# Gate and up products in two passes over a chunk, and new byte offsets for the low halves and the activations

## The reference, cut to what matters

```
def swiglu(x, w_gu, w_down):
    g, u = jnp.split(x @ w_gu, 2, axis=-1)
    return (jax.nn.silu(g) * u) @ w_down

for l in range(DEPTH):                       # DEPTH = 2
    f = swiglu(rms_norm(x, ffn1_pre_g[l]), ffn1_w_gu[l], ffn1_w_down[l])
    x = x + 0.5 * rms_norm(f, ffn1_post_g[l])
    ...                                      # hybrid mixer, then the second feed-forward
```

## Time and profile before

| | |
|---|---|
| median of 3 runs | 1475.48 us (1472.1 to 1476.35) |
| the profiled execution | 1471.1 us |
| its span, first to last instruction | 1469.0 us |
| TensorE busy | 1453.0 us, 99% of the span |
| VectorE busy | 1148.5 us, 78% |
| ScalarE busy | 767.2 us, 52% |
| DMA of the weight stream | 53.8% of 16 engines' span |
| mean granted TensorE clock | 0.994 |

### The profile page before, as it was taken

The page is one execution under the profiler, slowest core; times in us unless marked ns, Lnnn a source line. Parts: engine busy times, 40 slices in busy tenths (PEclk is TensorE's granted clock), DMA queues, the critical chain, the costliest instruction groups (busy, mean ns, idle before and its releaser), DMA issues.

```text
span 1469.0 us, 24487 instructions
## 1 busy us (share of the span) xinstructions
PE 1453.0 (99%) x8583; PEld 1266.1 (86%) x8583; DVE 1148.5 (78%) x1831; ACT 767.2 (52%) x1252; POOL 143.8 (10%) x140
## 2 busy tenths in 40 slices
PE   8999999999999999999999999999999999999999
PEld 7888889888888888889988888889988899888887
DVE  5777777878777777777787777878899987577876
ACT  6343476663434544337655434468498665453432
POOL 0000015200000000002420000020433310000000
PEclk9999999999999999999999999999899999999999
DMA  8665555546656666555555665656422356556652
GB/s 320 198 198 193 188 167 180 164 145 197 196 188 192 213 202 199 188 189 167 166 160 180 200 199 184 197 175 192 158 82 87 87 174 197 176 164 198 197 191 81
DMA packets 71361, 261.75 MB, mean 178 GB/s; under 512 B 8048, under 2 KB 8048, under 8 KB 71024
## 3 DMA queue, kind: packets, MB, share of 16 engines
q1 hardware_dynamic: 69984, 253.79, 53.8%
q10 hardware_dynamic: 1296, 6.85, 1.3%
HBM read 259.56 MB, written 1.05 MB: 177 GB/s over the span
## 4 chain that ended last, share of the span: by engine, by line
PE 92%; DVE 4%; ACT 2%; issue 1%; POOL 0%; DMA 0%; ACTq 0%; DVEq 0%
PE work L768 25%; PE work L769 13%; PE acc L481 9%; PE acc L483 9%; PE acc L482 9%; PE work L481 8%; PE work L483 7%; PE work L482 7%; DVE wlo L467 2%; PE work L1500 1%; PE acc L1529 1%; ACT whi L460 1%; PE acc L1565 1%; PE work L1501 0%; PE work L1488 0%
## 5 line engine op out<-in xcount | busy, mean ns | idle before, releaser
L467 DVE TENSOR_TENSOR wlo<-raw,whi 128x1024 fp32r<-128x1024 f32 x460 | 550.8, 1224 | 179.6 <-ACT whi L460 178.3
L768 PE MATMUL work<-xboth,whi 128*128 128x512 f32 x1600 | 564.2, 394 | 0.0
L460 ACT ACTIVATE whi<-raw 128x1024 fp32r<-128x1024 f32 x480 | 475.9, 1040 | 59.4 <-PE work L483 28.1
L769 PE MATMUL work<-xboth,wlo 128*128 128x256 f32 x1600 | 448.4, 280 | 0.0
L768 PEld LDWEIGHTS work<-xboth,whi 128*128 128x128 f32 x1600 | 300.8, 188 | 68.7
L769 PEld LDWEIGHTS work<-xboth,wlo 128*128 128x128 f32 x1600 | 299.8, 187 | 3.5
L846 ACT ACTIVATE sg<-sg 128x256 f32<-128x256 f32 x100 | 41.9, 419 | 474.6 <-DVE sg L887 474.6
L481 PE MATMUL acc<-whi,hhi 128*128 128x512 f32 x440 | 172.5, 392 | 0.0
L483 PE MATMUL acc<-whi,hlo 128*128 128x512 f32 x440 | 172.1, 391 | 0.0
L482 PE MATMUL acc<-wlo,hhi 128*128 128x512 f32 x440 | 171.1, 389 | 0.0
L481 PE MATMUL work<-xboth,whi 128*128 128x256 f32 x416 | 118.3, 284 | 0.0
(11 more groups left out here) (438 smaller groups left out, 2193.9 us busy)
## 6 DMA issues: line engine op xcount, KB each, us to landing
raw<-stream SPq DMA_DIRECT2D x480, 512.0 KB, 3.7
par<-pm ACTq DMA_DIRECT2D x2, 1644.5 KB, 7.4
pfa<-pf_a ACTq DMA_DIRECT2D x3, 516.0 KB, 3.7
pfb<-pf_b ACTq DMA_DIRECT2D x2, 516.0 KB, 8.4
x<-x_in SPq DMA_DIRECT2D x2, 512.0 KB, 5.9
out<-x SPq DMA_DIRECT2D x4, 256.0 KB, 2.0
par<-pm ACTq DMA_DIRECT2D x1, 820.0 KB, 4.3
pre<-pf_a ACTq DMA_DIRECT2D x1, 4.0 KB, 4.1
```

The lines of the kernel that those rows point to most:

```text
L460: nc.scalar.activation(chunk(whi, place, c)[:, cols], chunk(raw, place, c)[:, cols], ACT.Copy).then_inc(hi_ready, 1)
L467: nc.vector.tensor_tensor(chunk(wlo, place, c)[:, cols], chunk(raw, place, c)[:, cols], chunk(whi, place, c)[:, cols].bitcast(F32), ALU.su ...
L768: nc.tensor.matmul(o[:, :], hi[:, k * P:(k + 1) * P], xboth[:, k, :], start=k == 0, stop=False)
L769: m = nc.tensor.matmul(o[:, 0:S], lo[:, k * P:(k + 1) * P], xhi[:, k, :], start=False, stop=k == KD - 1)
```

## The change

Two edits. The loop of columns_of is cut in two: first the eight 512-column products of a chunk with the high weights, then the eight 256-column ones with the low weights. And unused 64-byte tensors are added or resized, so that each low part starts at another offset than its high part. From the sizes, the offsets modulo 128 after it are: whi 0, wlo 64, xboth (xhi and xlo) 0, hhi 0, hlo 64, yahi 0, yalo 64, mxhi 0, mxlo 64, and y5, cv and o at 64 as before. The number of instructions, the waits and the semaphore counts are the same.

```
@@ block_program, allocations @@
         whi = sb("whi", [P, RING * CH], F32R)
+        sb("low_line", [P, 16])
         wlo = sb("wlo", [P, RING * CH], F32R)
...
-        m1("hidden_line", [P, LINE])
+        m1("hidden_line", [P, 16])
         hhi = m1("hhi", [P, HELD, S], F32R)
+        m1("hidden_low_line", [P, 16])
         hlo = m1("hlo", [P, HELD, S], F32R)
...
-        m1("lru_line", [P, LINE])
-        yahi, yalo = m1("yahi", [P, AB, S], F32R), m1("yalo", [P, AB, S], F32R)
+        m1("lru_line", [P, 16])
+        yahi = m1("yahi", [P, AB, S], F32R)
+        m1("lru_low_line", [P, 16])
+        yalo = m1("yalo", [P, AB, S], F32R)
...
-        sb("state_line", [P, 16])
         y5hi, y5lo = sb("y5hi", [P, 4, S], F32R), sb("y5lo", [P, 4, S], F32R)
...
-        sb("mixed_line", [P, LINE // 2])
-        mxhi, mxlo = sb("mxhi", [P, KD, S], F32R), sb("mxlo", [P, KD, S], F32R)
+        sb("mixed_line", [P, 16])
+        mxhi = sb("mxhi", [P, KD, S], F32R)
+        sb("mixed_low_line", [P, 16])
+        mxlo = sb("mxlo", [P, KD, S], F32R)
@@ columns_of @@
                 for k in range(KD):
                     nc.tensor.matmul(o[:, :], hi[:, k * P:(k + 1) * P], xboth[:, k, :], start=k == 0, stop=False)
+                for k in range(KD):
                     m = nc.tensor.matmul(o[:, 0:S], lo[:, k * P:(k + 1) * P], xhi[:, k, :], start=False, stop=k == KD - 1)
                 m.then_inc(consumed, 1)
```

More of the change, by code:

```diff
@@ L38 @@
 VSTEPS = 49
-LINE = 32
 FFN_CHUNKS = 3 * FT
```

## The result

The changed kernel takes 1480.54 us, median of 8 runs, against 1473.0 us before, median of 8: a ratio of 1.0048, 95% interval 1.0037 to 1.0059. By the ratio it is 7.1 us slower; the prediction, 11.7 us faster and at most 1478, was wrong. (The 1464 us stood on a median before of 1475.48 us, of three runs; eight gave 1473.0.)

What follows compares the result with a forecast made beforehand. The prediction took TensorE's pace of starting products alone to bound the kernel. Its terms, -8.8 - 0.8 - 2.1 = -11.7 us, gave 1459.4 us in a profiled execution and 1464 us as a median, range 1452 to 1478.

Steps and rivals of the forecast that it cites:

- What bounds the kernel: Whole kernel: time comes only from TensorE's pace of starting products; other engines can follow a pace 3% higher.
- The offsets: All products: 512-column runs with moved and loaded operand both at 0 modulo 128 settle at 226.7 ns; unlike offsets may not.
- new first pass: Gate and up loop, eight 512-column products: 229.1 ns each, bounds 226.7 and 233.
- The second pass: Gate and up loop, 256-column products with low weights: 115.4 ns each, bounds 113.1 and 120.
- The pair: Gate and up, one 512- and one 256-column product: 344.5 ns against 350, -8.8 us; bounds -16.3 and +4.8.
- Down: Down and held products: like offsets stay like, so less is lost to settling, -0.8 us; bounds -1.7 and +6.2.
- tokens: 512-column products of tokens: two of three come from 233 to 226.7 ns, -2.1 us; bounds -3.2 and 0.
- channels: 256-column products of channels: possible gain of 5.0 us or loss of 2.7 us, taken as 0.
- y5, cv and o: These operands stay where they are; no time change was entered for their products.
- Products reach the best pace when the same kind follows itself: All products: best pace comes after three to seven of one kind; alternating 512 and 256 columns in gate and up prevents it.
- the slower one: Rival: low halves at 64 keep gate, up and down runs from settling, +7.9 us, 1483 us; chance 0.14.

Runs made afterwards that it cites:

- The series: Kernels with the whole computation left out: runs of products at chosen byte offsets, nothing on other engines; 512 columns took 226.7 to 233.3 ns a product.
- order, x -64: Kernel before with the two-pass loop, low halves at their high halves' offsets, xboth 64 bytes before the weights modulo 256: 1467.08 us, ratio 0.995.
- the locked kernel: Kernel before, one pass, low weights and activations 64 past the high weights, hidden high half 192 past, hidden low half at 0: 1465.6 us, ratio 0.9948.
- order, x +64: Kernel before with the two-pass loop, xboth moved by 64 bytes, each low half at its high half's offset: 1477.42 us, ratio 1.0022.
- order alone: Kernel before with the loop in two passes and all offsets as before: 1472.82 us, ratio 0.9991.

## Why the prediction was wrong, point by point

**What bounds the kernel** was right: TensorE's pace alone; no wait appeared, and the other engines followed a kernel 7.7 us faster without one.

**The offsets (the step that failed).** The prediction put down, output projections and the new first pass into one class: "moved and loaded operand both start at 0 modulo 128". The series know such a class modulo 256 only. From the sizes modulo 256, with whi put at 128 (the differences are what matters), hhi, hlo and mx lie at 128 too in the kernel before, xboth at 192 and y5, cv and o at 64; the change put xboth at 0 and the low halves at 192. So the first pass moves 0 and loads 128, half a period apart, and the series alone with these two offsets runs at 233.3 ns: the kernel has 233.4 where 229.1 was predicted (bounds 226.7 and 233). The second pass moves 0 and loads 192; its series runs at 117.8, the kernel at 117.6, predicted 115.4. The pair came to 351.0 where 344.5 was predicted and 349.8 measured before: +2.0 us for -8.8, inside the bounds of the term.

**Down.** "Like offsets stay like offsets" pairs a moved operand with the weights loaded for the next product. Of the operands that a product itself multiplies, two of three pairs come 64 apart: L482 moves wlo over hhi, L483 moves whi over hlo. The series of down products alone go against the prediction's pairing: 226.7 ns with all alike, 231.2 with both low halves 64 further, where that pairing has like offsets throughout, and 231.8 or 231.1 with one of them moved alone. Measured +2.0 us, for -0.8, inside the bound of +6.2. Output projections, priced within it, lost 0.7. Why such a run doesn't settle is not shown.

**tokens**: -0.4 for -2.1. In series of 24 and more its 512-column products settle at 231.3 to 231.4 ns after the change, from 233.3; two of three were to come to 226.7. Whi lies 128 and wlo 192 past xboth, not level with it, and single series at these distances run at 233.3. **channels**: +2.3 for 0, by the bound of +2.7; 1.3 of it is pace (its two long series run at 116.7 ns in place of 113.4), 0.9 clock. **y5, cv and o**: +2.0 where the prediction said that they stay as they are. Their own offsets did, but the low weights that they load moved under them, a term left out altogether; no bound of the sum had it. All four kernels whose low weights lie 64 further lose these 2.0 us; of the three others, two lose nothing and order, x -64 loses 1.7.

**Reading the rows.** The rows showed channels at two paces with the same operands and offsets; the prediction read it and still priced each kind by its own offsets. "Products reach the best pace when the same kind follows itself" is refuted: the passes of the changed kernel repeat the same kind eight times and don't reach it, tokens never did, and in the locked kernel 512 and 256 columns alternate at 227 and 114 ns. Order was not what kept gate and up from it.

The rival that came true is the slower one, with +7.1 us for its +7.9. Its mechanism was half right: the low halves at 64 cost 4.7 us in down, y5, cv and o and the output projections, which are back at their old times with low and high together (order, x +64), but in the gate and up loop 3.0 of the first pass's 3.9 us come from xboth, not from the low halves. That its number is so near is partly luck: the terms it named, gate, up and down, gave 4.0 us for its 7.9, and the rest came from kinds that it had at nothing.

The Trainium skill, "TensorE: Matmul & The Clock Gate", section "Step-by-step: what each phase is for", has the loading of weights take nothing from the running product, through ports of their own. The series do not bear that out: at fixed columns and clock the pace goes from 226.7 to 233.3 ns by the distance of the two operands' addresses alone, and it changes with the width of the load. What collides inside the chip no run here shows.

## What to carry to other kernels

In this kernel, bound by TensorE's pace, the byte offsets of stationary and moved operands modulo 256 moved the time by 0.5% either way, and a padding tensor changes them for everything behind it and for all that is paired with it. Such a choice can't be priced from classes of rows; run the whole repeating turn of products alone, with its real addresses, which here gave the kernel's distances to 1 ns, and pick by that. Test a placing in its sequence and not in a series of its own, and over more than two turns, since some placings change over in the third. Before two sums from profiled executions are compared, compare their time at the lower clock.

## What the runs showed that was not expected

- The pace of a series repeats with 256 bytes of difference between moved and loaded operand: 226.7, 228.8, 233.3, 233.3 ns for 512 columns at 0, 64, 128, 192, and 120.0, 117.8, 119 to 120, 113.3 for 256 (but for one placing).
- 32 bytes of difference cost 512 columns as much as the worst, some 233.4 ns, and 256 columns run at 116.7.
- The same series of channels, at the same addresses in the same kernel, ran once at 113.3 and once at 117.8 ns (order alone).
- A 64-byte move of an operand of the down products decides between 5.44 and 5.60 us for the 32 gate and up products before the next down chunk.
- A stationary operand of 32 columns in place of 128 makes a 512-column product slower where the offsets are equal, 231.7 in place of 226.7 ns.
